# The attentions of the first block, written out head by head in lockstep, become units of one-engine stages on a scheduler

## The reference

```
def mixer_layer(x, mem, layer_idx, ...):
    h = rmsnorm(x, g_norm);  z = h @ w_in          # 1024 x 13312
    dq, dk, dv, dg, lq, lk, lv, lg, mq, mg, mgate = split(z)
    # differential: 8 heads, two maps (m = 0, 1) of 64 dims each
    s = einsum('bqmhd,bkmhd->bmhqk', dq, dk) * 64**-0.5 + bias
    p = softmax(s);  w = p[:, 0] - lam * p[:, 1];  o_a = rmsnorm(w @ dv) * (1 - lam_init)
    y_a = (o_a * silu(dg)) @ w_br_diff
    # dilated: 4 heads over 3 groups, softmax joined over the groups
    y_b = (o_b * silu(lg)) @ w_br_dil
    # memory: 4 heads of 128 dims over 256 memory rows
    y_m = (softmax(mq @ mk) @ mv * silu(mg)) @ w_br_mem
    merged = sum of sigmoid(mgate)[i] * y_i
    return x + merged @ w_out
```

## Time and profile before

| | us |
|---|---|
| median of three executions | 2334.94 |
| the profiled execution | 2333.78 |
| its span | 2332.0 |
| TensorE busy in the span | 2198.4 (94%) |
| VectorE busy in the span | 1566.8 (67%) |
| ScalarE busy in the span | 1025.4 (44%) |

### The profile page before, as it was taken

How to read it: one execution, slowest core, us unless ns; L and a number is a source line. 1 busy time by engine, 2 the same in 40 slices (tenths; PEclk the granted TensorE clock), 3 DMA queues, 4 the chain that set the end, 5 groups by cost and what they waited for, 6 DMA issues and landing times.

```text
span 2332.0 us, 34030 instructions
## 1 busy us (share of the span) xinstructions
PE 2198.4 (94%) x13827; PEld 1956.4 (84%) x13827; DVE 1566.8 (67%) x2153; ACT 1025.4 (44%) x1682; POOL 174.7 (7%) x200
## 2 busy tenths in 40 slices
PE   6999998799999989989999999899999999999997
PEld 5999887688998877767899887799888899778996
DVE  5566767756667677665788758788744895656544
ACT  4444444444544444445433453433445434444433
POOL 1000000200000001110100100101100001110000
PEclk8999999899999999999999999999999999999999
DMA  8967665466766756442599642589643696524561
GB/s 286 289 197 233 213 228 187 165 237 203 218 218 224 243 188 204 167 149 69 187 315 323 209 166 91 171 309 321 221 159 100 208 341 213 182 92 163 183 206 64
DMA packets 305521, 474.56 MB, mean 204 GB/s; under 512 B 20416, under 2 KB 168330, under 8 KB 305364
## 3 DMA queue, kind: packets, MB, share of 16 engines
q1 hardware_dynamic: 295252, 440.68, 56.2%
q0 software_dynamic: 10112, 31.71, 4.6%
HBM read 465.88 MB, written 6.42 MB: 203 GB/s over the span
## 4 chain that ended last, share of the span: by engine, by line
PE 81%; DVE 9%; ACT 4%; issue 3%; POOL 1%; DMA 1%; SPq 0%; DVEq 0%; POOLq 0%; ACTq 0%
PE G L138 63%; PE A L138 16%; DVE pool L158 2%; PE G L141 2%; DVE wlo L150 1%; DVE S L158 1%; DVE pool L150 1%; ACT pool L144 1%; PE A L141 1%; POOL sm L150 1%; ACT S L144 1%; ACT whi L144 1%; DVE sm L161 1%; DVE X L150 1%; DMA pool<-in_mem 0%
## 5 line engine op out<-in xcount | busy, mean ns | idle before, releaser
L150 DVE TENSOR_TENSOR wlo<-raw,whi 128x1024 fp32r<-128x1024 f32 x640 | 771.4, 1233 | 239.0 <-ACT whi L144 237.0
L144 ACT ACTIVATE whi<-raw 128x1024 fp32r<-128x1024 f32 x640 | 645.1, 1053 | 165.3 <-DMA raw<-in_ffn_w_gu 97.2
L138 PE MATMUL G<-HTh,whi 128*128 128x256 f32 x2304 | 661.9, 287 | 4.6 <-ACT pool L144 4.6
L138 PE MATMUL G<-HTh,wlo 128*128 128x256 f32 x2304 | 652.9, 283 | 0.0
L138 PE MATMUL G<-HTl,whi 128*128 128x256 f32 x2304 | 652.7, 283 | 0.0
L138 PEld LDWEIGHTS G<-HTh,whi 128*128 128x128 f32 x2304 | 442.5, 192 | 10.0 <-issue 7.2
L138 PEld LDWEIGHTS G<-HTl,whi 128*128 128x128 f32 x2304 | 442.7, 192 | 2.5
L138 PEld LDWEIGHTS G<-HTh,wlo 128*128 128x128 f32 x2304 | 442.4, 192 | 0.0
L144 ACT ACTIVATE pool<-G 128x512 f32<-128x512 f32 (+3 forms) x208 | 115.3, 573 | 590.4 <-PE G L138 542.1
L138 PE MATMUL G<-whi,HTh 128*128 128x512 f32 (+1 forms) x768 | 309.7, 403 | 14.0 <-ACT HTh L144 10.8
L138 PE MATMUL G<-whi,HTl 128*128 128x512 f32 (+1 forms) x768 | 299.3, 390 | 3.2 <-DVE HTl L158 2.9
(11 more groups left out here) (195 smaller groups left out, 2343.9 us busy)
## 6 DMA issues: line engine op xcount, KB each, us to landing
raw<-in_ada_w SPq DMA_DIRECT2D x192, 512.0 KB, 5.7
raw<-in_ffn_w_gu SPq DMA_DIRECT2D x352, 256.0 KB, 4.9
raw<-in_w_in SPq DMA_DIRECT2D x224, 256.0 KB, 4.2
raw<-in_w_in SPq DMA_DIRECT2D x96, 512.0 KB, 5.0
raw<-in_ffn_w_down SPq DMA_DIRECT2D x88, 512.0 KB, 6.6
pool<-mod_rows POOLq DMA_DIRECT2D x24, 512.0 KB, 6.2
raw<-in_swa_w_in SPq DMA_DIRECT2D x24, 512.0 KB, 5.4
raw<-in_gla_w_in SPq DMA_DIRECT2D x24, 512.0 KB, 4.9
```

Source lines behind the costliest of these rows:

```text
L138: return self.e.matmul(out, a, b, start=start, stop=stop, skip_group_check=True) if self.e else self
L144: return self.e.activation(out, a, func, bias=bias, scale=scale, accum_out=accum) if self.e else self
L150: return self.e.tensor_tensor(out, a, b, op) if self.e else self
```

## The change

The lockstep `step()` and `drain()` go. In the first block each layer now sits down on the scheduler before the memory heads' gemms, with the two slots as seats (`three=False`) and one spare G bank, and it rises before `ya`.

```diff
         B = self.mkvb.pop(0)
+        self.sit((4, 6), 1, False)
         B["q"], B["g"] = self.mk_blk(4), self.mk_blk(4)
...
+        tail = [("ACT", "hi", 0, 0.4, -1), ("DVE", "lo", 0, 0.45, -1)]
+        ops = [("PE", "lg", 0, 0.95, -1), ("DVE", "max", 0, 0.9, -1), ("ACT", "exp", 0, 1.0, -1), ("DVE", "w", 0, 0.9, -1),
+               ("PE", "tr", 0, 0.5, -1), ("ACT", "cp", 0, 0.62, -1), ("PE", "pv", 0, 0.9, -1), ("DVE", "o", 0, 0.45, -1)] + tail
         for h in range(4):
-            self.pend.append(Unit("mem", 8, ("mem", l, h), h=h, B=B, st=st))
+            self.pend.append(self.queue("mem", ("mem", l, h), ops, self.clk["PE"] + 0.7, h=h, B=B, st=st,
+                                        there=lambda what: True))
...
+            ops = []
+            for t in range(2):
+                ops += [("PE", "lg", t, 1.35, -1), ("DVE", "max", t, 2.3, -1), ("ACT", "exp", t, 1.0, -1), ("DVE", "w", t, 0.85, -1),
+                        ("PE", "tr", 2 * t, 0.5, -1), ("ACT", "cp", 2 * t, 0.62, -1), ("PE", "tr", 2 * t + 1, 0.3, len(ops) + 4),
+                        ("ACT", "cp", 2 * t + 1, 0.4, -1)]
+            ops += [("PE", "pv", 0, 2.65, -1), ("DVE", "o", 0, 0.45, -1)] + tail
```

A dilated head's six transposes of one query half went into its own pair of banks with one copy of 768 columns; now four and two go into one G bank each, with a copy each. The differential heads:

```diff
-            vb = self.mk_blk(4)
-            gemm(HT, 0, ("diff", l, hf, 2), D, "TT", self.ev_copy(vb))
-            gb = self.mk_blk(4)
-            hs = {"g": gb, "out": [], "n": 0}
-            gemm(HT, 0, ("diff", l, hf, 3), D, "TT", self.ev_silu(gb))
-            for h in range(4 * hf, 4 * hf + 4):
-                self.pend.append(Unit("diff", 9, ("diff", l, h), l=l, h=h, q=qb, k=kb, v=vb, hs=hs))
+            vb, gb = self.mk_blk(4), self.mk_blk(4)
+            hs = {"g": gb, "out": [], "u": hf, "st": to, "free": lambda: blocks["free"]}
+            ops = [("PE", "lg", 0, 0.95, -1), ("DVE", "max", 0, 2.75, -1), ("ACT", "exp", 0, 1.9, -1), ("DVE", "w", 0, 2.1, -1),
+                   ("PE", "tr", 0, 0.5, -1), ("ACT", "cp", 0, 0.62, -1), ("PE", "pv", 0, 0.9, -1), ("ACT", "sq", 0, 0.6, -1),
+                   ("DVE", "oc", 0, 0.45, 7), ("DVE", "mean", 0, 0.25, 8), ("DVE", "y", 0, 1.9, 10)]
+            for h in range(4 * hf, 4 * hf + 4):
+                self.pend.append(self.queue("diff", ("diff", l, h), ops, self.clk["PE"] + 0.7, l=l, h=h, q=qb, k=kb, v=vb, hs=hs,
+                                            there=lambda what, x={"pv": vb, "y": gb}: len(x[what].tok) == 2))
+            gemm(HT, 0, ("diff", l, hf, 2), D, "TT", self.ev_copy(vb))
+            gemm(HT, 0, ("diff", l, hf, 3), D, "TT", self.ev_silu(gb))
...
+        blocks["free"] = True
         gbs = [gate_of(0, u) for u in range(2)]
-        self.drain(lambda: not self.busy())
-        for hf in range(2):
-            vb, gb, hs = V[hf]
-            rel = self.to_T(lambda t: vb.a[:, t * 512:t * 512 + 512], [[hs["out"]]] * 2, Sub(OT, 4 * hf), nk=4)
+        self.rise()
```

The logits of a differential head now take the two maps from different row halves and write them to different banks. For this the columns of dq and dk are put in another order when `w_in` is laid out for the launch, so q and k of a half are one run of 512 columns each and not two of 256:

```diff
-        add(("diff", l, hf, 0), wi, D, [(hf * 256, 256), (512 + hf * 256, 256)])
+        add(("diff", l, hf, 0), wi, D, [(hf * 512, 512)])
...
             for t in range(2):
                 for m in range(2):
-                    mm = e.matmul(sl.ps[:, t, m * 256:m * 256 + 256], q[p0:p0 + 64, m, j // 2, t * P:t * P + P],
-                                  k[p0:p0 + 64, m, j // 2, :], True, True)
+                    c = j * 256 + t * P
+                    mm = e.matmul(lg[:, m, t * 256:t * 256 + 256], u["q"].a[64 * m:64 * m + 64, c:c + P],
+                                  u["k"].a[64 * m:64 * m + 64, j * 256:j * 256 + 256], True, True)
```

More of the change, by code:

```diff
@@ L483, in mk_blk, with fits @@
     def mk_blk(self, n):
[L485 to L491, removed]
+        def fits():
+            return any(not any(self.pbusy[k:k + n]) for k in range(NB - n + 1)) and (
+                self.pbusy.count(False) >= n + 2 or not self.busy())
+        if self.seats and self.busy() and not fits():
+            self.advance(lambda: fits() or not self.busy())
+        return Blk(self, n)
     def busy(self):
         return bool(self.pend) or bool(self.loose) or any(x is not None for x in self.live)
[L497 to L512, removed]
     def spend(self, engine, us, ready=0):
@@ L561, in advance @@
                 engine, what, kc, us, after = u["ops"][u.s]
-                if what in ("pv", "y") and not u["there"]():
+                if what in ("pv", "y") and not u["there"](what) or what == "tr" and u.kind == "bring" and not u["there"]():
                     continue
-                at, bank = max(u["ends"][after] + 0.1, self.clk[engine]), None
+                at, bank = max(u["ends"][u.s if after < 0 else after] + 0.1, self.clk[engine]), None
                 if what in ("lg", "tr", "pv", "d", "s", "x"):
@@ L577, in advance @@
             u["ends"].append(self.spend(engine, us, at))
-            {"four": self.four, "bring": self.bring, "gla": self.gla, "fin": self.fin}[u.kind](u, *u["ops"][u.s][1:3], bank)
+            {"four": self.four, "bring": self.bring, "gla": self.gla, "fin": self.fin, "mem": self.mem, "dil": self.dil,
+             "diff": self.diff}[u.kind](u, *u["ops"][u.s][1:3], bank)
             u.s += 1
@@ L660, in tick @@
             self.advance()
[L661 to L668, removed]
     def fetch(self):
@@ L1056, in mem, with get_bias @@
[L1056 to L1063, removed]
-            u["tmp"] = self.blk(1)
-        self.h_mem(u)
-        if i == 7:
+    def get_bias(self, u):
+        u["bias"] = []
+        for i, h in enumerate([u["h"]] if u.kind == "diff" else [8 + gi * 4 + u["h"] for gi in range(3)]):
+            r = 3 * u["j"] + i
+            src = bass.AP(self.M.scratch.tensor, h * P * 512 + 127, [[511, P], [1, 384]])
+            ev = (f"bias{r}", (u.name, i))
+            self.h_bias(r, src, self.scr[0], self.bias_free[r], ev)
+            u["bias"].append((r, ev))
```

476 lines of the change are left out of this document (246 added, 230 removed).

## The result

Seven executions of the changed kernel took 2343.76 to 2354.16 us, median 2346.11; seven of the kernel before beside them 2333.01 to 2336.53, median 2335.78. The ratio is 1.0052 (95% interval 1.0037 to 1.0067): 10.3 us slower, where 26 us faster was predicted. The profiled execution took 2352.25, 6.1 above its median.

What follows compares the result with a forecast made beforehand. TensorE, busy 94% of the span, was taken as the bound. Logits -13.8, waits -25, insertions +3, banks +7 and bias +3 sum to -25.8 from 2333.8, giving 2308.0 us; range 2279 to 2331.

Steps and rivals of the forecast that it cites:

- The logits: First block's 16 heads: each logit group 0.86 us shorter as row halves overlap, 13.8 us less in TensorE's stream.
- R3: Rival: the logits' 13.8 us doesn't show, as halves don't overlap or logits wait for VectorE; 2322 us, chance 0.05.
- (a): First stop of both layers: comes within hf = 1's v gemm, only the last two heads' ends left; 12 us less.
- R2: Rival: waits move and don't go, heads held back and run out at the next stop or before `ya`; 2328, chance 0.20.
- (b): Second stop of layer 0, costing 10.1 us: last two heads still lack their exponentials; 4 us less.
- (c): Wait of 6.3 us for the memory rows behind layer 0's second stop: load order stays, 0.
- (d): Stop of layer 1, costing 4.7 us: heads done just in time before the layer rises; 4 us less.
- (e): Remaining short waits on S and a bank, with low clock, 9.9 us: stages issued when input is planned ready; 5 less.
- Banks: Transposes or products holding a G bank make three FF gemm starts a layer wait, six of 1.2 us; 7 us more.
- R4: Rival: held G banks make FF starts wait; the change loses from 14 such starts, 2349 us with 20; chance 0.08.
- Insertions (+3), bias (+3), loads (0): Dilated transposes split between gemm matmuls, 3 us more; VectorE waiting for `bias_t`, 3 more; larger q and k loads, 0.
- The second block: Everything after the first block: must take as long as before, 0.

Runs made afterwards that it cites:

- experiment 1: Kernel before with the row halves alone (weight order, logits and map layout as changed, units in the old order): 2325.94 us.
- experiment 4: Changed kernel with only differential heads on the scheduler, memory and dilated heads in the old lockstep, second block's banks as before: 2322.77 us.
- experiment 3: Changed kernel with one bank skipped in the rotation after the first block's second layer, giving the second block its old banks: 2343.66 us.
- experiment 12: Fastest kernel of experiment 11 with both maps of a head in one row half: 2313.62 us; or with differential heads' pieces in G banks: 2301.54 us.
- experiment 10: 48 pool blocks and seven raw buffers: on experiment 5 2321.37 us, on the kernel before 2323.71, on experiment 8 2310.52.
- experiment 11: Experiment 10's 2310.52 us kernel with memory rows a gemm later 2302.62 us; margin 1.0 us too 2316.60; lockstep with row halves, 48 blocks 2319.90; all heads scheduled 2316.29.
- experiment 5: Changed kernel with the first block's transposes and value products in A banks alone, second block's banks as before: 2320.84 us.
- experiment 8: Experiment 4 with the transposes and value products in A banks alone: 2318.89 us.

## Why the prediction was wrong, step by step

In medians, along the kernel before, experiments 1, 4 and 3, and the changed kernel: row halves -9.4, differential heads on the scheduler -3.2, memory and dilated heads on it +20.9, the second block's banks +2.4. That is 10.7; the changed kernel's own set, with the kernel before 0.5 us higher, has 10.3. The -3.2 and the +2.4 are within their intervals.

**The logits (-13.8).** Right in kind and in the row: 1.06 us to the next instruction, as predicted, but only 9.4 in time. The step that failed is "these lie in TensorE's stream itself, so nothing hides them": a transpose behind the logits waits for VectorE, so before a wait the saved 0.86 lengthens the wait. R3 had this and was given 0.05; 4.4 of the 13.8 are missing, and the waits on S grew by 5.3. Where few stops are left (experiment 12) 2.8 are still missing, so waits at the stops may not be all of it.

**(a) The first stop (-12).** Failed. Its place was right (both layers, within the v gemm of hf = 1). The length was not: 7.41 and 0.69 us idle in layer 0, 7.9 in layer 1, against 2.5 left with the clock. The step that failed is "no longer two heads from their logits". In layer 0 the logits of two heads stand right at the stop, and VectorE is busy for 7.67 of the next 8.30 us; in layer 1 a head's logits stand within it (874.19), between waits of 2.68 and 3.88 us. By the kernel file's plan the two are the last head of the first half and the first of the second: the stop issues whatever the plan has next, also the sum, maximum and maps of a head that holds none of the blocks that are wanted, and VectorE does part of them before the maps that TensorE waits for. What it would bring to force only the head that frees blocks was not tried. Experiment 10 shows that a stop taken away comes back where blocks are next asked for; experiment 11, that most of it goes if both places go: R2's "waits move", in the form of a later stop.

**(b), (c), (d).** Right, (b) by its sign. (b): 5.5 us idle (4.82 + 0.69) and, at 0.79 of the clock over 9.66 busy us, 2.0 more: 7.5 where I left 6.1, so 2.6 of the 4 came. (c): the memory rows' wait stayed, 6.2. (d): behind its first stop layer 1 has no wait of over 1.9 us before `ya`. (R2's "99%" for layer 1 is 29.8 of 31.8, 94%.)

**(e) The short waits (-5).** Failed in sign. A stage "issued when its input is planned ready" has 0.1 us of margin in a plan that does not know the gemms' evacuations on ScalarE and VectorE. So TensorE stands before a copy that ScalarE makes late: eleven waits of value products on ACT W, of 11.3 us, where before there were two of 0.7. The lockstep gave each stage a whole gemm piece. This term stays with A banks: in experiment 11 the waits on ACT W and on the scores in the memory and dilated stages are 11.4 us with these heads on the scheduler (4.1 and 1.2 in layer 0, 3.2 and 2.9 in layer 1) and 1.6 without, which is most of the 13.7 that they cost there. With much the same waits they cost only 2.0 by the medians of experiments 5 and 8, so what the waits are worth in time is shown for one order only.

**Banks (+7).** With (a) the largest error. Six waits of 1.2 us were reckoned, all at gemm starts; there are 15 of 16.5 us, six of them pieces that wait for a bank a gemm has just left, a direction I did not count. Taking the G banks away brought 22.8 us. That is R4: its 14 starts at 2.4 us each are 15 at 1.5 (22.8 / 15), if all of the 22.8 is put down to them; the plan's times changed with the banks too, and this was not separated. It got 0.08 because "the second block works so", and there the heads have three seats and other neighbours; experiment 12 confirms that the neighbours decide, but not which.

**Insertions (+3), bias (+3), loads (0).** The bias cost nothing: VectorE's wait for `bias_t` was 1.0 us in layer 0's differential stage before and is 0.3 after (the 4.5 in the earlier trace rows are waits for the logits). The insertions were not measured alone; in the traces of experiment 11 TensorE is busy for 3.5 us longer in the memory and dilated stages with these heads on the scheduler, the clock's part included. No wait on the loads appeared.

**The second block (0).** Wrong by 2.4 us in the medians, which is within the intervals; but in the traces a stretch around the gated linear stage (1394 to 1606 us before) takes 218.5 and 218.7 us in the two kernels with the shifted banks and 210.2 to 213.2 in the 18 others. The rotation of the G banks runs through the whole program, and an edit in the first block shifted it. No line of the diff says so.

## What to carry to other kernels

A stage that an in-order engine reaches too early costs that engine its wait, whatever the plan says; so before lockstep is given up for a plan, hold the plan's margins against everything that the other engines do in between, evacuations included. Count the buffers that the main stream rotates through before letting side work take one, in both directions (main waits for side, side waits for main), and keep the rotation the same when one part is measured. A stall for memory lasts until the work that holds the memory is through, together with whatever else is issued into it, and it moves to the next request when it is removed; look for that request first, and for what the stall issues that frees nothing.

## What the runs showed of the hardware that was not expected

The memory and dilated stage of layer 0 took 213.9, 214.1, 215.9 and 216.0 us in the profiled executions of four kernels with the same instructions and buffers there, while that of layer 1 took 238.2 in all of them. So 2 us of difference in one trace of the first stretch tell nothing. The rest of the program, with the same gemms in the same banks, took 1360.8 to 1368.6 us in nine such traces with eight raw buffers: nor do 8 us there.
